# First mixer of a two-block network on one core: query rotation, bonus, decays and the first block of an inverse put in another order

## The reference

```python
def even_layer(h, ...):
    u = rmsnorm(h, norm_mix)
    proj = u @ w_in
    rw_cols, mla_cols = proj[..., :RW_COLS], proj[..., RW_COLS:]
    rw_prev = jnp.pad(rw_cols[:, :-1], ((0, 0), (1, 0), (0, 0)))
    rw_cols = rw_cols + shift_mu * (rw_prev - rw_cols)
    y_a = rwkv7_time_mix(*split_cols(rw_cols, RW_SIZES), ...)
    y_b = mla_attention(*split_cols(mla_cols, MLA_SIZES), ...)
    h = h + jnp.concatenate([y_a, y_b], axis=-1) @ w_out
    return h + swiglu(rmsnorm(h, norm_ffn), ffn_wg, ffn_wu, ffn_wd)

def rwkv7_time_mix(r, k, v, w_down, a_down, g_down, ...):
    log_w = -jax.nn.softplus(-(w0 + jnp.tanh(w_down) @ w2)) - 0.5
    a = jax.nn.sigmoid(a0 + a_down @ a2)
    g = jax.nn.sigmoid(g_down) @ g2
    # kk: k * k_k, normalised per head
    k = k * (1.0 + (a - 1.0) * k_a)
    # state (64 x 64 per head) over 256 steps:
    #   S_t = S_{t-1} (diag(w_t) - kk_t^T (kk_t * a_t)) + v_t^T k_t,  y_t = S_t r_t
    # y: group norm of y_t
    bonus = jnp.sum(r_h * k_h * r_k, axis=-1, keepdims=True) * v_h
    return (y + bonus) * g

def mla_attention(q_lat, kv_lat, k_rope, ...):
    q = to_heads(rmsnorm(q_lat, q_norm) @ w_uq, h)     # the last 32 of 96 columns are rotated
    kv = to_heads(rmsnorm(kv_lat, kv_norm) @ w_ukv, h) # keys get the rotated k_rope appended
    out = block_causal_attention(q, k, v, scale)
```

## Time and profile before

| | |
|---|---|
| median of 3 runs | 1979.77 us (1979.73 to 1981.44) |
| the profiled execution | 1980.34 us, its span 1978.4 us |
| TensorE busy | 1889.4 us, 96% of the span |
| VectorE, ScalarE, GpSimd busy | 1466.5, 1140.0, 39.3 us |
| chain that ended last | TensorE 87%, VectorE 7%, ScalarE 4%, issue 2% |
| mean granted clock of TensorE | 0.969 |
| 0 to 165 us | TensorE busy 125.95 us, granted clock 0.91 |
| 165 to 262 us | TensorE busy 92.79 us, granted clock 0.95 |

### The profile page before, as it was taken

One profiled execution on the slowest core, in us unless ns is written; L12 is line 12 of the kernel. 1 busy time (PEld: TensorE's weight loads), 2 busy tenths in 40 slices (PEclk: granted clock), 3 DMA queues, 4 the chain that ended last, 5 costly groups with the idle time before them and its releaser, 6 DMA issues.

```text
span 1978.4 us, 28126 instructions
## 1 busy us (share of the span) xinstructions
PE 1889.4 (96%) x11217; PEld 1639.4 (83%) x11217; DVE 1466.5 (74%) x1543; ACT 1140.0 (58%) x1239; POOL 39.3 (2%) x84
## 2 busy tenths in 40 slices
PE   7878999999999899999999999999999998989998
PEld 6757889999977788888888888888888886979987
DVE  4677746555743588988889889898898887597585
ACT  5532234334343576767777677676776776646653
POOL 0020000000011000000000000000000000000010
PEclk9899989999987899999999999999999999989999
DMA  7200034555410588989889899898998988324431
GB/s 320 86 0 1 1 134 167 189 186 177 145 69 1 240 346 348 362 334 369 359 338 365 331 372 363 337 375 326 371 354 342 370 349 328 134 93 147 149 128 44
DMA packets 64208, 467.44 MB, mean 236 GB/s; under 512 B 7248, under 2 KB 7376, under 8 KB 7888
## 3 DMA queue, kind: packets, MB, share of 16 engines
q1 hardware_dynamic: 64080, 465.66, 60.7%
HBM read 464.58 MB, written 1.05 MB: 235 GB/s over the span
## 4 chain that ended last, share of the span: by engine, by line
PE 87%; DVE 7%; ACT 4%; issue 2%; POOL 0%; DMA 0%; SPq 0%; DVEq 0%; ACTq 0%
PE bank L551 84%; PE bank L561 2%; DVE split_ring L1868 2%; ACT arena L1339 1%; ACT split_ring L1339 1%; ACT late_high L1339 0%; ACT L1339 0%; DVE arena L1899 0%; ACT operand_high L1339 0%; DVE arena L1900 0%; POOL arena L2672 0%; DVE arena L1878 0%; DMA parameters<-param_dram 0%; ACT moe_pair_high L1339 0%; DVE arena L1902 0%
## 5 line engine op out<-in xcount | busy, mean ns | idle before, releaser
L2429 DVE TENSOR_TENSOR moe_pair_low<-weight_ring,moe_pair_high 128x2048 fp32r<-128x2048 f32 x225 | 506.9, 2287 | 13.2 <-ACT moe_pair_high L1339 13.1
L1339 ACT ACTIVATE moe_pair_high<-weight_ring 128x2048 fp32r<-128x2048 f32 x225 | 426.5, 1917 | 35.0 <-DMA weight_ring<-w_dram 33.8
L551 PE MATMUL bank<-moe_pair_high,operand_high 128*128 128x512 f32 x896 | 353.4, 394 | 4.4 <-DVE operand_low L2436 3.4
L551 PE MATMUL bank<-moe_pair_high,operand_low 128*128 128x512 f32 x896 | 352.7, 394 | 0.0
L551 PE MATMUL bank<-moe_pair_low,operand_high 128*128 128x512 f32 x896 | 350.0, 391 | 0.0
L551 PE MATMUL bank<-operand_high,split_ring 128*128 128x256 f32 x1536 | 331.1, 288 | 8.6 <-DVE split_ring L1868 8.2
L1339 ACT ACTIVATE arena<-bank 128x256 f32<-128x256 f32 (+4 forms) x209 | 90.4, 440 | 373.0 <-PE bank L551 337.6
L551 PEld LDWEIGHTS bank<-operand_high,split_ring 128*128 128x128 f32 x1536 | 259.0, 194 | 12.8 <-DVE split_ring L1868 10.7
L551 PEld LDWEIGHTS bank<-moe_pair_high,operand_high 128*128 128x128 f32 x896 | 168.7, 188 | 39.8 <-issue 3.6
L551 PEld LDWEIGHTS bank<-moe_pair_high,operand_low 128*128 128x128 f32 x896 | 168.4, 188 | 38.0
L551 PEld LDWEIGHTS bank<-moe_pair_low,operand_high 128*128 128x128 f32 x896 | 168.8, 188 | 36.8
(11 more groups left out here) (313 smaller groups left out, 3215.0 us busy)
## 6 DMA issues: line engine op xcount, KB each, us to landing
weight_ring<-w_dram SPq DMA_DIRECT2D x381, 1024.0 KB, 6.9
arena<-w_dram SPq DMA_DIRECT2D x55, 1024.0 KB, 4.9
constants<-const_dram SPq DMA_DIRECT2D x1, 3124.0 KB, 17.7
parameters<-param_dram SPq DMA_DIRECT2D x1, 2896.5 KB, 25.5
hT<-x_dram SPq DMA_DIRECT2D x1, 1024.0 KB, 4.8
out_dram<-squares SPq DMA_DIRECT2D x4, 256.0 KB, 2.1
constants<-const_dram SPq DMA_DIRECT2D x1, 128.0 KB, 4.6
parameters<-param_dram SPq DMA_DIRECT2D x1, 54.5 KB, 4.4
```

Source lines behind the costliest of these rows:

```text
L551: return pe.matmul(out, lhsT, rhs, start=start, stop=stop, skip_group_check=True)
L1339: return act.activation(out, in_, f, **kw)
L2429: tt(low_, raw_, high_.bitcast(F32), ALU.subtract).then_inc(moe_split, 1)
```

## The change

It changes the order of the first mixer at five places and nothing that is computed:

1. x has a semaphore of its own. VectorE squares x (four operations of 512) ahead of its low parts; ScalarE no longer does, and it runs a one-element copy first, so that its table load stands ahead of the wait for x.
2. TensorE does three projections ahead of the low-rank products instead of two. `hi(2)` and `lo(2)` stand ahead of the lerp of slot 6, the copy ahead of the tanh, and the gate's products alone wait for the sigmoid.
3. The third lerp and the fifth weight's high and low part (`hi(4)`, `lo(4)`) come one slot ahead: ScalarE does `hi(3)`, `hi(4)`, then the lerp, and VectorE's decays stand behind all three.
4. The partner matmuls stand between the query and key products, one pair behind its queries, each waiting only for that pair's evacuation. VectorE rotates three pairs, adds the first keys, rotates the last pair and adds the other keys. The bonus matmuls and their products, and Bs, move into the attention (heads 0, 2 and 1), and KR's first half from head 3 to 4.
5. In the first block `level_block(0, 0)` stands ahead of `first_turned(0)`, and TensorE waits for the turned form only ahead of the second group of products.

```diff
@@ -248,2 +248,3 @@
 
+        x_landed = sem("residual_landed")
         loaded = sem("inputs_loaded")
@@ -673,3 +674,3 @@
 
-            pe.wait_ge(loaded, 48)
+            pe.wait_ge(loaded, 32)
             pe.wait_ge(S["zero_ready"], 1)
@@ -693,5 +694,6 @@
             project(V)
+            project(V)
             pe.wait_ge(tables_loaded, 32)
-            pe.wait_ge(S["lora_in"], 2)
-            for w, x in ((Pm("wa2"), lw), (Pm("wa2"), lx), (Pm("g2"), sg)):
+            for w, x, inputs in ((Pm("wa2"), lw, 2), (Pm("wa2"), lx, 2), (Pm("g2"), sg, 3)):
+                pe.wait_ge(S["lora_in"], inputs)
                 for j2 in range(2):
@@ -704,3 +706,2 @@
             project(V)
-            project(V)
             pe.wait_ge(S["kk_sq"], 1)
@@ -729,2 +730,8 @@
 
+            def partners(j2, evacuated):
+
+                pe.wait_ge(A.freed, evacuated)
+                bank = V.claim(pe)
+                V.fill(mm(bank[:, :], C("partner_mla"), qh[:, 2 * j2:2 * j2 + 2, :]))
+
             for j2 in range(NH // 2):
@@ -736,2 +743,5 @@
                 queries = A.fill(last)
+                if j2:
+                    partners(j2 - 1, queries - 1)
+
             for j2 in range(NH // 2):
@@ -741,3 +751,5 @@
                     last = mm(bank[:, j * T:(j + 1) * T], wukv[:, cc:cc + P], kvl)
-                V.fill(last)
+                keys = V.fill(last)
+                if j2 == 0:
+                    partners(NH // 2 - 1, queries)
             pe.wait_ge(S["lerp_out"], 7)
@@ -749,8 +761,11 @@
             pe.wait_ge(S["bonus_in"], 1)
-            for j2 in range(2):
-                bank = V.claim(pe)
-                V.fill(mm(bank[:, 0:512], C("same_head"), sq_[:, 1024 + j2 * 512:1024 + (j2 + 1) * 512]))
-            pe.wait_ge(A.freed, queries)
-            rope(qh, NH, "mla")
             pe.wait_ge(S["rope_done"], 1 + NH // 2)
+            pe.wait_ge(V.freed, keys)
+
+            def bonus(i):
+
+                if i in (0, 2):
+                    at = 1024 + i * 256
+                    bank = V.claim(pe)
+                    V.fill(mm(bank[:, 0:512], C("same_head"), sq_[:, at:at + 512]))
 
@@ -760,3 +775,3 @@
 
-            attention(mla_scores, vml, 0)
+            attention(mla_scores, vml, 0, bonus)
 
@@ -810,3 +825,4 @@
             for a in range(TT):
-                pe.wait_ge(S["first_inverse"], a + 1)
+                if a:
+                    pe.wait_ge(S["first_inverse"], 2)
                 dj = [V.np, V.np]
@@ -829,2 +845,4 @@
                         spread(0)
+                    if a == 0 and n == 0:
+                        pe.wait_ge(S["first_inverse"], 1)
                     for h4 in range(2):
@@ -1399,7 +1417,8 @@
 
-            act.wait_ge(loaded, 48)
+
+            st.lone(a_(tiny[:, 153:154], zcol, ACT.Copy))
+            act.wait_ge(x_landed, 16)
+            act.wait_ge(loaded, 32)
             for n in range(4):
                 h_parts(0, n)
-            for n in range(4):
-                h_squares(0, n, sq_)
             hi(0)
@@ -1407,2 +1426,3 @@
             hi(1)
+            hi(2)
             act.wait_ge(S["mix_ready"], 1)
@@ -1424,7 +1444,5 @@
             lerped(6, 0)
-            hi(2)
             act.wait_ge(S["lerp_out"], 1)
+            st.say(a_(lx[HD:P], rw_dl[HD:P, 0, :], ACT.Copy), "lora_in")
             st.say(a_(lw[0:HD], rw_dl[0:HD, 0, :], ACT.Tanh), "lora_in")
-            st.lone(a_(lx[HD:P], rw_dl[HD:P, 0, :], ACT.Copy))
-            st.settle()
             st.say(a_(sg, rw_dl[:, 1, :], ACT.Sigmoid), "lora_in")
@@ -1446,4 +1464,4 @@
             hi(3)
-            lerped(3, 2)
             hi(4)
+            lerped(3, 2)
             act.wait_ge(S["lerp_out"], 3)
@@ -1891,3 +1909,3 @@
 
-            def rope(x, n, tables, ta, tb):
+            def rope(x, n, tables, ta, tb, first=0):
 
@@ -1895,3 +1913,3 @@
                 ta, tb = chunks(ta, 2), chunks(tb, 2)
-                for c in range(0, n, 2):
+                for c in range(first, n, 2):
                     bank = V.take(dve)
@@ -1960,3 +1978,7 @@
 
-            dve.wait_ge(loaded, 48)
+            dve.wait_ge(x_landed, 16)
+            for n in range(4):
+                cols = slice(2 * n * T, (2 * n + 2) * T)
+                st.say(tt(sq_[:, cols], hT_[:, cols], hT_[:, cols], ALU.mult), "sq_piece")
+            dve.wait_ge(loaded, 32)
             for n in range(4):
@@ -1992,4 +2014,4 @@
             mix_in(0)
-            lerped(6, 0)
             lo(2)
+            lerped(6, 0)
             mix_in(1)
@@ -1997,2 +2019,5 @@
             lerped(2, 1)
+            mix_in(2)
+            lo(4)
+            lerped(3, 2)
             dve.wait_ge(A.freed, done["lora", "w0"])
@@ -2008,5 +2033,2 @@
             st.own(tt(cs8, cs8, mid.rearrange("p (n o) -> p n o", o=1).broadcast_to([P, 8, P]), ALU.subtract))
-            mix_in(2)
-            lo(4)
-            lerped(3, 2)
             st.lone(tt(csx, cs, logd, ALU.subtract))
@@ -2073,3 +2095,5 @@
             kpe2 = kpe.rearrange("p (o t) -> p o t", o=1).broadcast_to([P, 2, T])
-            for j2 in range(NH // 2):
+            mla_tables = C("cos_mla"), C("sin_mla")
+
+            def keys_in(j2):
 
@@ -2077,10 +2101,9 @@
                 V.free(tt(kh[:, 2 * j2:2 * j2 + 2, :], bank[:, :].rearrange("p (c t) -> p c t", c=2), kpe2, ALU.add))
-            dve.wait_ge(S["exp_out"], 1)
-            st.own(tt(Bs, kk, iclr, ALU.mult))
-            dve.wait_ge(A.freed, done["v_turned"])
-            for j2 in range(2):
-                bank = V.take(dve)
-                v2 = rw_v[:, 2 * j2:2 * j2 + 2, :]
-                V.free(tt(v2, v2, bank[:, :].rearrange("p (c t) -> p c t", c=2), ALU.mult))
-            rope(qh, NH, (C("cos_mla"), C("sin_mla")), rt1, rt2)
+
+            st.wait_said("lerp_out")
+            rope(qh, NH - 2, mla_tables, rt1, rt2)
+            keys_in(0)
+            rope(qh, NH, mla_tables, rt1, rt2, first=NH - 2)
+            for j2 in range(1, NH // 2):
+                keys_in(j2)
 
@@ -2090,5 +2113,14 @@
 
-                if i == 1:
-                    st.own(tt(Bs, Bs, E3, ALU.mult))
+                if i in (0, 2):
+                    if i == 0:
+                        dve.wait_ge(A.freed, done["v_turned"])
+                    bank = V.take(dve)
+                    v2 = rw_v[:, i:i + 2, :]
+                    V.free(tt(v2, v2, bank[:, :].rearrange("p (c t) -> p c t", c=2), ALU.mult))
+                elif i == 1:
+                    dve.wait_ge(S["exp_out"], 1)
+                    st.own(tt(Bs, kk, iclr, ALU.mult))
                 elif i == 3:
+                    st.own(tt(Bs, Bs, E3, ALU.mult))
+                elif i == 4:
                     st.own(tt(KR[:, :, :, 0, :], v4(kk), v4(E2), ALU.mult))
@@ -2164,4 +2196,4 @@
             first_level()
-            first_turned(0)
             level_block(0, 0)
+            first_turned(0)
             for a in range(TT):
@@ -2677,3 +2709,3 @@
         def _(sp):
-            sp.dma_start(hT_[:, :], x_dram).then_inc(loaded, 16)
+            sp.dma_start(hT_[:, :], x_dram).then_inc(x_landed, 16)
```

More of the change, by code:

```diff
@@ L1992, in _ @@
             mix_in(0)
+            lo(2)
             lerped(6, 0)
-            lo(2)
             mix_in(1)
@@ L2164, in _ @@
             first_level()
+            level_block(0, 0)
             first_turned(0)
-            level_block(0, 0)
             for a in range(TT):
```

4 lines of the change are left out of this document (2 added, 2 removed).

## The result

The changed kernel takes 1969.57 us (median of 8 runs, 1964.29 to 1975.11); the kernel before took 1980.43 beside it (8 runs, 1978.53 to 1985.46). The ratio is 0.9947, with an interval of 0.9929 to 0.9964: 10.9 us faster, against 10.0 forecast. The profiled execution took 1968.86 us, with a span of 1967.0.

A forecast was written before the change was run, and what follows sets the result against it. TensorE's chain was taken as the bound, in the first mixer waiting for weight splits, rotated queries and the inverse's first level factor. 5.9 + 4.8 - 2.65 + 0.4 + 1.5 = 10.0 us off 1979.77 gave 1969.8, range 1965.5 to 1975.0.

The forecast's parts named there:

- The first projection: Start of the mixer: TensorE first projects at 14.8 instead of 17.00, 2.2 us saved, with VectorE the later engine.
- The new wait: Behind the low-rank products, ending at 37.8: TensorE waits 4.9 us for the fourth weight's split, until 42.7.
- The ninth projection: End of the projections: starts at 85.0 instead of 90.92, 5.9 us earlier (5.3 to 6.4), the start's saving included.
- the key latent: Its scaling on VectorE, at 63.32 before: taken at 57.4; VectorE's queue gives 57.0, TensorE 56.4 to 57.9.
- The rotation: Query rotation before the attention: logits start at 111.1 instead of 121.68, 4.8 us beyond the 5.9; TensorE waits 1.4.
- the 2.65: Attention: Bs and two bonus products moved onto a VectorE without gaps lose 2.65 us.
- The inverse: First block of the inverse: TensorE's first products start 2.9 us earlier, of which 1.5 is gained (1.1 to 1.9).
- The sum: All parts: 5.9 + 4.8 - 2.65 + 0.4 + 1.5 = 10.0 us, median 1969.8.
- (b): Rival, attention: GpSimd's scaling sets the pace, 4.5 us more lost, gain 5.5, 1974.3; chance 0.17 with (a) and (c).
- (c): Rival, projections: the low-rank order only moves the stall, gain 6.3, 1973.5; chance 0.17 with (a) and (b).
- (a): Rival, TensorE's clock: more half-clock time eats part, gain 6, 1973.8; chance 0.17 with (b) and (c).
- (e): Rival, later program: another busy half-clock stretch costs 12.6 us, making the kernel slower by 2.6; chance 0.04.

The follow-up runs named there:

- third_undone: Changed kernel with only two projections ahead of the low-rank products again, and their inputs ordered as before: 1971.45 us beside 1971.40.
- bonus_ahead: Changed kernel with the bonus matmuls, their products and Bs ahead of the attention again: 1969.21 us (one run, beside 1985.48).
- fifth_alone: Kernel before with only the fifth weight's parts and the third lerp one slot ahead of the decays: 1979.84 us (one run, beside 1985.48).

## Why the prediction was right, point by point

**The first projection:** 14.8 forecast, 14.68 measured, with VectorE as the later engine: x lands at 5.70, low parts end at 11.39, split from 12.34.

**The new wait:** the low-rank products end at 37.41 (37.8) and project again at 42.27 (42.7), a wait of 4.9 as forecast. The lead at that point is as computed. What the prediction missed is why the third projection pays. It holds that the move removes the 2.7 for ScalarE's inputs; with the shorter start the landing of the parameters would have taken 3.5 in its place (third_undone).

**The ninth projection:** 85.0 forecast, 83.87 and 84.36 measured: a lead of 7.0 in the profile pair, where 5.9 was summed. The mis-sized term is the key latent, 57.4 in the sum and 56.27 in the trace. The sum charged TensorE 2.9 us of half clock behind the new wait. The stretch at half clock did come, and yet the row has no idle time before it: VectorE set the time, not TensorE. VectorE's own queue was forecast to reach it at 57.0, and was 0.7 quicker. This is the half-clock stretch, beside which VectorE is busy 6.72 of 6.8 us:

```profile
40.50:47.30 6.80, 5.03 (x23) 5.03 (x24) 6.72 (x8) 3.81 (x8) 0.00 (x0) 0.50 0.03 11
```

It is a near thing, though. In the second profile of the changed kernel the half-clock stretch begins 1.1 us later, and VectorE waits for TensorE after all:

```profile
56.77 0.69 DVE L1943 TENSOR_TENSOR ycat<-bank,arena 128x512 f32<-128x512 f32 x1 [0.57 <-PE bank L552]
```

So the prediction's mechanism, TensorE behind its new wait, held in one of the two profiles, and there it was 0.6 us too dear.

**The rotation:** the first logits start at 109.81 on TensorE, 11.9 earlier than in the earlier trace rows, of which 7.0 are the projections' and 4.8 the rotation's, as forecast. TensorE waits 1.8 (1.4). But the 4.8 was measured against a profile with 6.8 us at half clock from 121.0 and as much from 90.2. Against the average of all six profiles of the old order the part is worth 1.7 net at A8, not 2.55, and 0.6 against the two with no half clock behind P9. In the profile pair the lead grew from 7.0 at P9 to 10.3 at A8, which is 4.8 + 0.8 − 2.35. Given back in the attention were 2.35 of the 2.65, since VectorE was busy 14.38 of 14.8 us; the 0.8 is what the first logits won by full clock (0.4 forecast): VectorE takes them 0.9 us behind TensorE's start, and 1.8 before. Both can be read in the stretches of before, at the first logits, and of the changed kernel, over the attention:

```profile
121.00:127.80 6.80, 5.50 (x17) 4.24 (x17) 4.85 (x11) 1.97 (x8) 1.72 (x2) 0.50 0.00 0
```

```profile
110.70:125.50 14.80, 10.34 (x60) 6.58 (x60) 14.38 (x35) 7.41 (x28) 7.69 (x10) 1.00 0.00 1
```

The prediction took the idle 2.8 us of TensorE as room and saw none on VectorE, which held; it did not see that VectorE waits 1.2 us for the first logits, which is where the bonus belongs (bonus_ahead). Its 4.8 was also 0.1 too much by its own numbers: 121.68 − 5.9 − 111.1 is 4.7.

**The inverse:** 1.5 forecast, 1.3 to 2.4 measured, with a wait of 3.1 for the level factor in place of 6.0.

**The sum:** 7.0 + 1.7 + about 1.9 (the middle of the two bounds) is 10.6, beside 10.9 in the medians. That the 10.0 lay near it is partly luck, in that the projections were 1.1 too small and the rotation 0.9 too large.

That the sum of the parts meets the medians is partly luck too. From VectorE's first subtraction of a level to E both kernels run the same order. The two profiles of before take 103.6 and 105.3 us for it, the three of the changed kernel 102.5, 99.7 and 101.2. So the average lead is 11.2 us at that subtraction, close to the parts' 10.6, and 14.5 at E, with times 14.3 apart; the medians are 10.9 apart. No part accounts for the 3.3 us between. TensorE stands idle 4.2 us there in both profiles of before and 4.2 to 5.0 in the changed kernel, so it isn't a wait; it is the clock, at half speed for 10.2 and 14.0 us of it before and for 10.2, 3.4 and 6.8 us after.

**The rivals.** (b) and (c) are excluded by bonus_ahead and fifth_alone, though (c) is right of the third projection alone. (a), that the clock eats part of the gain, did not show: in the first 270 us the two profiles of before have 41.0 and 51.2 us at half clock, and the three of the changed kernel 27.3, 17.1 and 27.3. If anything the clock helped, and how much of the 10.9 us it gave stays open. Between two executions of one kernel E moved by 4.4 and 4.9 us. Whether the clock favours one of them on average the profiles can't settle, with two of the kernel before and three of the changed one; the medians are 10.9 and 9.6 us apart in the two timed batches, where the sum of the parts is 10.6. (e) did not come about: the mean granted clock was 0.967 to 0.975 in the changed kernel's eight runs, and its time follows it (1975.11 at 0.967, 1964.29 at 0.975).

## What to carry to other kernels

Price a part of a reordering with the others in place: the third projection gained nothing alone (0.6 to 1.9 us later) and gained 0.5 to 1.4 in company, because which wait ends last had changed. When an engine with no gaps in a stage is to take on work, look for the microsecond in which it waits for that stage's first result, just ahead of it. And take a second profile of the kernel before, if one can be had, ahead of computing a gain from the first: one term here was taken from a stretch that ran at half clock in one execution and not in others.

## What the runs showed of the hardware that I had not expected

Most of the half-clock stretches do not stay with the instructions. The first projections and waits of two executions repeat to some tenths of a microsecond, and then the attention's tail takes 7.6 us in eight profiles and 9.9 to 10.4 in six, with one and the same order of instructions. The Trainium skill (TensorE: Matmul & The Clock Gate, "The HAM clock gate") calls the gate free-running; the two profiles of the changed kernel fit that, with clock 0.50 in one and 1.00 in the other from 129.2 to 136.0 us.

One stretch does go with the order. In all six profiles in which TensorE stands 5.7 us for the rotated queries, the clock falls to 0.50 within that wait (at 121.0 in the first) and stays there for 6.8 us. In the six in which it stands 1.8 us there, it doesn't fall in or right behind that wait. That the shorter wait is the cause is likely but was not tested apart.

A single time of this kernel can be 5 us off its median, and a single profile is good for the long waits and for who releases them, less for lengths: for the key latent even the releaser changed between two profiles.
